# A two-pass form of 44 projection units, with the low half copied by ScalarE and added by VectorE

## The chip, the cores and the metric

The kernel runs on one core of a Trainium2 chip. The metric is the device time of one execution in microseconds (us); it was measured in 3 runs, and the median is 1423.44 us. One execution was also recorded by the hardware profiler. Times within the trace count from the start of its span.

## The reference, cut to what matters

A sequence of 256 tokens with 1024 channels goes through two layers of one kind of block and then through a block of another kind, the **third block**. All is float32. Its mixing stage begins like this (the splits are of one projection):

```python
h = rmsnorm(x, norm_mix)
proj = h @ w_in                      # 1024 -> all projections
(z, xbc, dt_raw, lru_y, lru_x, q, k, v, ret_g, gate_pre) = jnp.split(proj, offsets, axis=-1)
xbc = silu(causal_dwconv(xbc, conv_w, conv_b))          # four taps
xb  = causal_dwconv(lru_x, lru_conv_w, lru_conv_b)      # four taps
...                                  # gates r, i from xb; u; an associative scan gives hs
y_lru = hs * gelu(lru_y)
qh, kh = rotary(q), rotary(k)        # retention
y_ret = norm(retention(qh, kh, v)) * silu(ret_g)
```

The three branch outputs (state space, LRU, retention) are each multiplied by a branch matrix, gated, summed, projected and added to x, and a feed-forward with a three-tap convolution follows.

## The kernel before, in words

**Numbers in two halves.** Every matrix product is made of rounded operands: a value is split in a high half (rounded to the format of TensorE) and a low half (what is left), and a product is high x high + low x high + high x low. All weights come in *units* of 128 x 1024 values. There are 461 units, in a ring of four buffers: SyncE loads `raw`, ScalarE rounds it to `w_hi` (`high`, L502 to L512, 1024 columns in one instruction), GpSimd subtracts to get `w_lo` (`low`, L477 to L481, in two halves), TensorE uses both and signals `unit_done`. `high` for a unit waits until TensorE is done with the unit four places earlier; ScalarE issues it inside its own hand-written order, between its other work.

**A projection unit.** `linear_unit` (L1204) makes 128 output channels for 256 tokens: 8 blocks of 128 input channels, and for each three matmuls of 256 columns (`mm3`, L1191 to L1193), 24 in all, into a *slot*. The four slots are the first halves (256 columns) of PSUM banks 4 to 7, used in turn. Before it writes a slot, TensorE waits for `slot_free` or `act_free`, which the engine that read the slot last gives. The activations' halves lie side by side in the buffer `both`: per block 256 columns high, then 256 columns low. `up_unit` (L1217) is the same product in another form, used in the feed-forwards: 8 matmuls of 512 columns multiply `w_hi` with both halves at once, so that the low part arrives in the second half of the bank (`low_part`), and 8 of 256 columns add `w_lo` x high to the slot (L1223, L1225). There ScalarE copies the low part to SBUF (`copy_low`, L584) and VectorE adds it to the slot (`add_low`, L1863). A PSUM bank is 512 columns wide.

**The order of the third block's mixing stage.** Each engine runs a list written out by hand; nothing is planned by a program. TensorE's order is:

1. 8 units for `lru_x`, one for dt (a `linear_unit`), 12 for `xbc`. For each of the 20, ScalarE takes the slot (`take`, L890: first a `high`, then the wait for the unit), writes middle tap times slot plus bias to SBUF (`middle_tap`, L899) and VectorE adds the three shifted taps from the slot (`shifted_taps`, L2232, three dependent instructions), then frees the slot with a small memset (L2238). Beside this, VectorE subtracts to get low halves (`parts_low`, L2281) and works out a softplus in small steps (L2247 to L2276); ScalarE makes the high halves (L903) and the Silu of finished `xbc` channels (L928). After the ninth `xbc` unit TensorE makes a cumulative sum that waits for the softplus result (L1606), which ScalarE copies out two units later.
2. Four rounds: one unit of the LRU's gates in four parts of six matmuls, each part with its own slot (Tanh by ScalarE, L970), four transposes (L1631), and one query unit. VectorE copied the query slot to `qk` right after the unit (L2329). In the same round run, in this order: VectorE L2319, L2326; ScalarE `decays` (L957 Exp, L960 Tanh); VectorE L2331, L2334. The fourth part of a gate unit uses the slot of the query unit before it.
3. Four key units (copied by VectorE, L2338), with square roots on ScalarE (L995), VectorE's products (L2345) and eight scans (L2349) beside them.
4. 8 units for `lru_y`: Gelu by ScalarE (L1013), product by VectorE (L2358), high and low half of it (L903, L2281).
5. Gate and branch products, the value and state-space stage, 8 units for `z`.
6. 8 units for `ret_g` (`gate_high`, Silu by ScalarE, L1049), with small products of the retention between them; VectorE here scales eight tiles (L2455) and makes their low halves (L2460).
7. The remaining gate and branch products and the output projection, then the feed-forward.

Of the kernel before, what the change touches and what calls it, by code (L numbers as in the profile page):

```python
# [154 lines left out]
def program(nc, t, per_trip, found, blocks=3):  # L155
    with ExitStack() as ctx:
# [335 lines left out]
        def _(act):  # L492
# [402 lines left out]

            def middle_tap(dst, tap, bias):
                s = take()
                act.wait_ge(init, 1)
                act.activation(dst, slot(s), ACT.Identity, scale=tap, bias=bias)\  # L899
                    .then_inc(pre_ready, d.inc(pre_ready))  # L900
# [62 lines left out]
            for b in range(4):  # L963
# [10 lines left out]
                d.skip(unit_done)  # L974
                next_slot()
                decays(b)

# [6 lines left out]
            for q in range(4):  # L984
                high()
                d.skip(unit_done)
                next_slot()
                load_segments(q)
                if q == 0:
                    act.wait_ge(m2_ready, d.next(m2_ready, 4))  # L990
                if q < 2:
                    for k in (2 * q, 2 * q + 1):
                        if k >= 2:
                            act.wait_ge(root_out, d.next(root_out))
                        act.activation(bank(2 + k % 2), a2("r", 2 * k * T, 2 * T), ACT.Sqrt, scale=0.25)\  # L995
                            .then_inc(root_ready, d.inc(root_ready))
# [51 lines left out]
            def gate_high(c):  # L1048
                act.activation(a2("xdt", c * T, T), slot(take()), ACT.Silu).then_inc(act_free, d.inc(act_free))  # L1049
# [130 lines left out]
        def _(pe):  # L1180
# [36 lines left out]
            def up_unit():  # L1217
# [3 lines left out]
                pe.wait_ge(slot_free, d.next(slot_free))  # L1221
# [48 lines left out]
            def last_two(hi, lo, c, ready):  # L1270
# [10 lines left out]
                token_rows(other, hi, lo, c + 1, 1, True).then_inc(unit_done, d.inc(unit_done))  # L1281

# [297 lines left out]
            linear_unit(h_hi, h_lo, hlo_ready)  # L1580
            for _ in range(3):
                linear_unit(h_hi, h_lo)
# [12 lines left out]
            for _ in range(CH - RING + 1):  # L1595
                linear_unit(h_hi, h_lo)
            for c in range(SSD_T):
                linear_unit(h_hi, h_lo, free=None if c == 3 else slot_free)
# [15 lines left out]
            for b in range(4):  # L1614
# [18 lines left out]
                linear_unit(h_hi, h_lo, free=act_free)  # L1633
            linear_unit(h_hi, h_lo, free=act_free)
            linear_unit(h_hi, h_lo, free=act_free)
# [7 lines left out]
            linear_unit(h_hi, h_lo, free=act_free)  # L1643
            linear_unit(h_hi, h_lo)
# [28 lines left out]
            for c in range(CH):  # L1673
                linear_unit(h_hi, h_lo, free=slot_free if c < RING else act_free)
# [71 lines left out]
            for h in range(RET_H):  # L1746
                linear_unit(h_hi, h_lo, free=act_free)
# [8 lines left out]
                linear_unit(h_hi, h_lo, free=act_free)  # L1756
# [59 lines left out]
        def _(dve):  # L1816
# [408 lines left out]

            def shifted_taps(dst, s, name, c, per, taps, final):
# [59 lines left out]
            for c in range(CH):  # L2286
                s = take()
# [6 lines left out]
            for c in range(SSD_T):  # L2294
                s = take()
# [17 lines left out]
            for b in range(4):  # L2313
# [8 lines left out]
                for half in range(2):  # L2322
# [5 lines left out]
                s = take()  # L2328
                dve.tensor_copy(a2("qk", b * T, T), slot(s)).then_inc(slot_free, d.inc(slot_free))  # L2329
# [5 lines left out]
                    .then_inc(m2_ready, d.inc(m2_ready))  # L2335
            for q in range(4):
                s = take()
                dve.tensor_copy(a2("qk", (RING + q) * T, T), slot(s)).then_inc(slot_free, d.inc(slot_free))  # L2338
# [13 lines left out]
            for c in range(CH):  # L2352
                d.skip(unit_done)
                next_slot()
# [5 lines left out]
                if c:  # L2360
                    parts_low(0, c - 1, bank(3 - c % 2, 0, T))
            parts_low(0, CH - 1, bank(3, 0, T))
# [393 lines left out]
```

## Time and profile before

| what | value |
|---|---|
| median of 3 runs | 1423.44 us (1423.15 to 1423.67) |
| the profiled execution | 1422.63 us, of which the span is 1420.8 us |
| TensorE busy | 1407.9 us, 99% of the span |
| GpSimd busy | 1183.3 us, 83% |
| ScalarE busy | 867.9 us, 61% |
| VectorE busy | 711.0 us, 50% |
| DMA | 256 MB, 180 GB/s |
| third block's mixing stage | about 830 to 1200 us of the span |

The times are sums over the whole span. An average of this kind hides that an engine may be early in one stage and the last to finish in another, so it has to be read stage by stage. The granted clock of TensorE is given as a share of its full speed.

### The profile page before, as it was taken

The page shows a single profiled execution, that of the slowest core. Times are in us where ns is not written, and L with a number is a line of the kernel's source. Part 1 is how long each engine was busy: PE and PEld are TensorE (multiplying, and loading weights), DVE is VectorE, ACT ScalarE, POOL GpSimd, SP SyncE. Part 2 cuts the span into 40 slices and gives each one's busy share as a digit, 9 for nine tenths or more (in the row PEclk, how much of TensorE's full clock was granted, in tenths as well). Part 3 has the DMA queues.
Part 4 walks back from the last instruction along what each step waited for, and adds up shares of the span by engine and source line. Part 5 has one row for each costly group of instructions (what it writes and reads, how often), then busy time and mean ns, then how long its engine had stood idle before and what let it go on. Part 6 is the DMA issues. An engine that isn't in the chain of part 4 may idle for free.

```text
span 1420.8 us, 25105 instructions
## 1 busy us (share of the span) xinstructions
PE 1407.9 (99%) x7866; PEld 1208.7 (85%) x7866; DVE 711.0 (50%) x1594; ACT 867.9 (61%) x1463; POOL 1183.3 (83%) x926
## 2 busy tenths in 40 slices
PE   9999999999999999999999999999999999999998
PEld 8877778888888777788888899998899888888887
DVE  4654454645555734446555565660863612544444
ACT  6655656666675655657666676854444545755555
POOL 5977687999969777888999979899676898799995
PEclk9999999999999999999999999999999999999999
DMA  7765455666557755565666656566544466566663
GB/s 255 222 189 151 135 183 158 199 201 191 186 171 209 225 155 145 165 179 159 207 191 192 190 179 193 165 204 198 167 141 134 151 207 184 163 200 193 192 188 93
DMA packets 140064, 256.09 MB, mean 180 GB/s; under 512 B 8192, under 2 KB 98896, under 8 KB 139600
## 3 DMA queue, kind: packets, MB, share of 16 engines
q1 hardware_dynamic: 128224, 244.61, 56.1%
q10 hardware_dynamic: 11760, 10.41, 2.8%
q8 instruction: 50, 0.82, 0.2%
q14 instruction: 30, 0.25, 0.1%
HBM read 253.89 MB, written 1.10 MB: 179 GB/s over the span
## 4 chain that ended last, share of the span: by engine, by line
PE 96%; DVE 2%; ACT 1%; DMA 0%; issue 0%; SPq 0%; ACTq 0%
PE psum L1191 21%; PE psum L1192 20%; PE psum L1193 20%; PE psum L1223 17%; PE psum L1225 9%; DVE arena L2405 1%; PE psum L1310 1%; PE psum L1376 1%; PE psum L1329 1%; PE psum L1320 1%; PE psum L1298 1%; PE psum L1689 0%; PE psum L1377 0%; PE psum L1337 0%; DMA arena<-in_x 0%; PE psum L1439 0%
## 5 line engine op out<-in xcount | busy, mean ns | idle before, releaser
L480 POOL TENSOR_TENSOR w_lo<-raw,w_hi 128x512 fp32r<-128x512 f32 x461 | 603.8, 1310 | 221.2 <-ACT w_hi L512 217.8
L512 ACT ACTIVATE w_hi<-raw 128x1024 fp32r<-128x1024 f32 x461 | 486.8, 1058 | 298.6 <-PE psum L1193 189.4
L481 POOL TENSOR_TENSOR w_lo<-raw,w_hi 128x512 fp32r<-128x512 f32 x461 | 610.4, 1324 | 0.0
L1223 PE MATMUL psum<-both,w_hi 128*128 128x512 f32 x1040 | 259.1, 391 | 0.0
L1223 PEld LDWEIGHTS psum<-both,w_hi 128*128 128x128 f32 x1040 | 190.7, 188 | 36.6
L1191 PE MATMUL psum<-w_hi,both 128*128 128x512 f32 (+1 forms) x544 | 212.3, 390 | 0.0
L1193 PE MATMUL psum<-w_lo,both 128*128 128x512 f32 (+1 forms) x544 | 205.7, 378 | 0.0
L1192 PE MATMUL psum<-w_hi,both 128*128 128x512 f32 (+1 forms) x544 | 205.4, 378 | 0.0
L1225 PEld LDWEIGHTS psum<-both,w_lo 128*128 128x128 f32 x1040 | 141.9, 190 | 10.1
L1863 DVE TENSOR_TENSOR psum<-psum,arena 128x256 f32<-128x256 f32 x136 | 58.6, 432 | 174.1 <-ACT arena L584 174.1
L1225 PE MATMUL psum<-both,w_lo 128*128 128x256 f32 x1040 | 145.0, 282 | 0.0
L1191 PE MATMUL psum<-both,w_hi 128*128 128x256 f32 x488 | 141.5, 290 | 0.0
L1193 PE MATMUL psum<-both,w_hi 128*128 128x256 f32 x488 | 138.0, 283 | 0.0
L1192 PE MATMUL psum<-both,w_lo 128*128 128x256 f32 x488 | 138.0, 283 | 0.0
L1191 PEld LDWEIGHTS psum<-w_hi,both 128*128 128x128 f32 x544 | 102.3, 188 | 27.0 <-issue 9.6
L1193 PEld LDWEIGHTS psum<-w_lo,both 128*128 128x128 f32 x544 | 102.4, 188 | 20.0
L1192 PEld LDWEIGHTS psum<-w_hi,both 128*128 128x128 f32 x544 | 102.5, 189 | 17.4
L1191 PE MATMUL psum<-w_hi,f_hi 128*128 128x512 f32 x272 | 106.7, 392 | 0.0
L1192 PE MATMUL psum<-w_hi,f_lo 128*128 128x512 f32 x272 | 106.6, 392 | 0.0
L1193 PE MATMUL psum<-w_lo,f_hi 128*128 128x512 f32 x272 | 105.8, 389 | 0.0
L1191 PE MATMUL psum<-w_hi,y_hi 128*128 128x512 f32 x256 | 101.0, 394 | 0.0
L1193 PE MATMUL psum<-w_lo,y_hi 128*128 128x512 f32 x256 | 99.8, 390 | 0.0
(291 smaller groups left out, 2156.8 us busy)
## 6 DMA issues: line engine op xcount, KB each, us to landing
raw<-in_units SPq DMA_DIRECT2D x453, 512.0 KB, 3.6
arena<-gate_rows ACTq DMA_DIRECT2D x8, 512.0 KB, 7.6
raw<-in_units SPq DMA_DIRECT2D x8, 384.0 KB, 3.0
arena<-in_bias ACTq DMA_DIRECT2D x2, 1024.0 KB, 5.0
arena<-acs_rows ACTq DMA_DIRECT2D x16, 128.0 KB, 3.9
arena<-in_consts ACTq DMA_DIRECT2D x1, 1296.0 KB, 6.0
raw<-in_units SPq DMA_DIRECT2D x8, 128.0 KB, 3.0
out<-arena SPq DMA_DIRECT2D x4, 256.0 KB, 2.7
```

What stands on the lines that cost most here:

```text
L480: pool.tensor_tensor(w_lo[s][:, 0:D // 2], raw[s][:, 0:D // 2], w_hi[s][:, 0:D // 2].bitcast(F32), ALU.subtract)
L481: pool.tensor_tensor(w_lo[s][:, D // 2:D], raw[s][:, D // 2:D], w_hi[s][:, D // 2:D].bitcast(F32), ALU.subtract)\
L512: act.activation(w_hi[s][:, :], raw[s][:, :], ACT.Copy).then_inc(hi_ready, d.inc(hi_ready))
L1191: pe.matmul(out, hi, r_hi, start=start, stop=False, **kw)
L1192: pe.matmul(out, lo, r_hi, start=False, stop=False, **kw)
L1193: return pe.matmul(out, hi, r_lo, start=False, stop=stop, **kw)
L1223: pe.matmul(bank(4 + k), blocks_of(w_hi[s], c), both[:, 2 * c * T:2 * (c + 1) * T], start=(c == 0), stop=False, skip_group_check=True)
L1225: last = pe.matmul(slot(k), blocks_of(w_lo[s], c), chunk(h_hi, c), start=False, stop=(c == CH - 1), skip_group_check=True)
L1298: last = pe.matmul(turned_chunk(c, half * P, P), tok(x, half, c * P, P), rows[:, half * P:(half + 1) * P], start=True, stop=True)
L1310: last = pe.matmul(bank(h, r * T, T), arena[lo:hi, at:at + P], arena[lo:hi, ak:ak + T], start=True, stop=True)
L1320: last = pe.transpose(bank(2, kc * T + r * P, P), sc[:, r * T + kc * P:r * T + (kc + 1) * P], ident)
L1863: dve.tensor_tensor(slot(k), slot(k), low_part(k)[1], ALU.add).then_inc(vec, d.inc(vec))
```

## The change

The units of steps 1 (without dt), 2, 3, 4 and 6 take the form of `up_unit`: 8 + 12 + 4 + 4 + 8 + 8 = 44. The dt unit, the `z` units, the gate and branch products stay. `up_unit` gets a parameter for the signal it waits for. The very first unit is written out with a wait before each block (`first_unit`).

What reads the slots changes with it. `take_sum` on ScalarE is `take`, then a copy of the low part to `pre` (SBUF), then a wait for VectorE's sum; `take_sum` on VectorE waits for that copy and adds it to the slot. It is used for the convolution units, the Gelu units and the Silu units; the operation on the slot follows the sum. For queries and keys ScalarE copies the slot (the high part) to `qk` (`query_part`) and VectorE adds the low part straight from PSUM (`query_sum`). In step 2 the query copy stands behind `decays`, and VectorE's addition at the end of its round instead of in its middle. In step 4 `parts_low` moves from behind the product to before it, one unit later.

```diff
+            def take_sum():            # ScalarE
+                s = take()
+                act.activation(chunk(pre, s), low_part(s)[0], ACT.Copy).then_inc(low_out, d.inc(low_out))
+                act.wait_ge(sum_ready, d.next(sum_ready))
+                return s
+            def query_part(c):
+                act.wait_ge(unit_done, d.next(unit_done))
+                act.activation(a2("qk", c * T, T), slot(next_slot()), ACT.Copy).then_inc(low_out, d.inc(low_out))
             def middle_tap(dst, tap, bias):
-                s = take()
+                s = take_sum()
...
-                d.skip(unit_done)
-                next_slot()
                 decays(b)
+                query_part(b)
...
                 high()
-                d.skip(unit_done)
-                next_slot()
+                query_part(RING + q)
                 load_segments(q)
...
-                    act.activation(a2("merged", c * T, T), slot(take()), ACT.Gelu_apprx_tanh).then_inc(act_free, d.inc(act_free))
+                    act.activation(a2("merged", c * T, T), slot(take_sum()), ACT.Gelu_apprx_tanh).then_inc(act_free, d.inc(act_free))
...
-                act.activation(a2("xdt", c * T, T), slot(take()), ACT.Silu).then_inc(act_free, d.inc(act_free))
+                act.activation(a2("xdt", c * T, T), slot(take_sum()), ACT.Silu).then_inc(act_free, d.inc(act_free))
...
+            def first_unit():          # TensorE
+                s = unit()
+                k = next_slot()
+                pe.wait_ge(slot_free, d.next(slot_free))
+                for c in range(CH):
+                    pe.wait_ge(hlo_ready, d.next(hlo_ready))
+                    pe.matmul(bank(4 + k), blocks_of(w_hi[s], c), both[:, 2 * c * T:2 * (c + 1) * T], start=(c == 0), stop=False, skip_group_check=True)
+                    last = pe.matmul(slot(k), blocks_of(w_lo[s], c), chunk(h_hi, c), start=False, stop=(c == CH - 1), skip_group_check=True)
+                last.then_inc(unit_done, d.inc(unit_done))
...
-                linear_unit(h_hi, h_lo, free=None if c == 3 else slot_free)
+                up_unit(free=None if c == 3 else slot_free)
...
-                linear_unit(h_hi, h_lo, free=act_free)
+                up_unit(free=act_free)
...
+            def take_sum():            # VectorE
+                s = take()
+                dve.wait_ge(low_out, d.next(low_out))
+                dve.tensor_tensor(slot(s), slot(s), chunk(pre, s), ALU.add).then_inc(sum_ready, d.inc(sum_ready))
+                return s
+            def query_sum(c):
+                s = take()
+                dve.wait_ge(low_out, d.next(low_out))
+                dve.tensor_tensor(a2("qk", c * T, T), a2("qk", c * T, T), low_part(s)[0], ALU.add).then_inc(slot_free, d.inc(slot_free))
...
-                s = take()
+                s = take_sum()
                 shifted_taps(a2("xbc", c * T, T), s, "ssd_conv", c, 5, 4, conv_done)
...
-                s = take()
-                dve.tensor_copy(a2("qk", b * T, T), slot(s)).then_inc(slot_free, d.inc(slot_free))
                 dve.wait_ge(a_ready, d.next(a_ready))
...
                     .then_inc(m2_ready, d.inc(m2_ready))
+                query_sum(b)
             for q in range(4):
-                s = take()
-                dve.tensor_copy(a2("qk", (RING + q) * T, T), slot(s)).then_inc(slot_free, d.inc(slot_free))
+                query_sum(RING + q)
...
             for c in range(CH):
-                d.skip(unit_done)
-                next_slot()
+                take_sum()
+                if c >= 2:
+                    parts_low(0, c - 2, bank(2 + c % 2, 0, T))
                 dve.wait_ge(act_free, d.next(act_free))
...
                 for _ in range(2):
-                    d.skip(unit_done)
-                    next_slot()
+                    take_sum()
                 dve.wait_ge(act_free, d.next(act_free, 2))
```

## Rows read from the trace of the kernel before

**Rows 1.** The page, part 4: the chain that ended last, by engine.
```profile
PE 96%; DVE 2%; ACT 1%; DMA 0%; issue 0%; SPq 0%; ACTq 0%
```
**Rows 2.** Windows: stretch, its length, busy time of PE, PEld, DVE, ACT, POOL; clock.
```profile
833.00:893.00 60.00, 60.00 (x496) 59.10 (x495) 36.09 (x100) 40.06 (x65) 55.60 (x44) 1.00 0.63 201
```
**Rows 3.** Waits of VectorE, 833 to 960: total us, times, longest.
```profile
DVE arena L2232 <- ACT arena L899: 23.3, 18, 4.9
```
**Rows 4.** Timeline of ScalarE, second convolution group: start, duration, line, operation.
```profile
868.07 1.28 ACT L928 ACT_TABLE_LOAD   x1
...
876.13 0.57 ACT L899 ACTIVATE arena<-psum,prm 128x256 f32<-128x256 f32 x1 [1.06 <-PE psum L1193]
...
876.90 1.05 ACT L512 ACTIVATE w_hi<-raw 128x1024 fp32r<-128x1024 f32 x1
879.01 0.57 ACT L899 ACTIVATE arena<-psum,prm 128x256 f32<-128x256 f32 x1 [1.06 <-PE psum L1193]
...
885.70 0.57 ACT L899 ACTIVATE arena<-psum,prm 128x256 f32<-128x256 f32 x1 [2.00 <-PE psum L1193]
```
**Rows 5.** Timeline of TensorE: the cumulative sum; two units of the feed-forward.
```profile
881.78 0.61 PE L1606 MATMUL psum<-arena 128*16 128x256 f32 x2
...
1264.66 1.98 PE L1223 MATMUL psum<-both,w_hi 128*128 128x512 f32 x8
...
1270.22 0.40 PE L1191 MATMUL psum<-w_hi,f_hi 128*128 128x512 f32 x1
```
**Rows 6.** Groups of instructions, whole span, then 833 to 893: busy us, mean ns.
```profile
L1863 DVE TENSOR_TENSOR psum<-psum,arena 128x256 f32<-128x256 f32 x136 | 58.6, 432 | 174.1 <-ACT arena L584 174.1
L584 ACT ACTIVATE arena<-psum 128x256 f32<-128x256 f32 x136 | 49.4, 367 | 3.7 <-PE psum L1225 3.7
...
L2268 DVE SCALAR_TENSOR_TENSOR rows<-rows,psum 128x40 f32<-128x40 f32 x7 | 1.4, 195 | 0.2
```
**Rows 7.** Timeline of VectorE: three taps, a low half, the longest softplus step.
```profile
844.70 1.52 DVE L2232 SCALAR_TENSOR_TENSOR arena<-psum,prm,arena 128x255 f32<-128x255 f32 x3 [1.36 <-ACT arena L899]
846.15 0.99 DVE L2281 TENSOR_TENSOR y_lo<-arena,y_hi 128x512 fp32r<-128x512 f32 x1
...
878.25 0.82 DVE L2272 SCALAR_TENSOR_TENSOR psum<-rows,rstd 128x40 f32<-128x40 f32 x1
```
**Rows 8.** Timeline of GpSimd: first half of the weights rounded at 876.90.
```profile
878.96 1.30 POOL L480 TENSOR_TENSOR w_lo<-raw,w_hi 128x512 fp32r<-128x512 f32 x1
```
**Rows 9.** Timelines of TensorE, ScalarE and VectorE, one gate round (907 to 915).
```profile
907.16 0.60 PE L1631 MATMUL psum<-common,arena 128*128 128x128 f32 x4
...
913.36 0.60 PE L1631 MATMUL psum<-common,arena 128*128 128x128 f32 x4
...
908.11 0.82 ACT L970 ACTIVATE arena<-psum,prm 128x256 f32<-128x256 f32 x2
...
910.47 1.10 ACT L957 ACTIVATE arena<-arena,small 128x256 f32<-128x256 f32 x2 [0.58 <-DVE arena L2319]
...
908.96 1.47 DVE L2319 SCALAR_TENSOR_TENSOR arena<-arena 128x512 f32<-128x512 f32 x1 [0.84 <-ACT arena L970]
...
911.60 1.81 DVE L2331 TENSOR_TENSOR psum<-arena 128x512 f32<-128x512 f32 x1 [0.17 <-ACT arena L957]
913.44 0.69 DVE L2334 SCALAR_TENSOR_TENSOR arena<-psum,arena 128x512 f32<-128x512 f32 x1
```
**Rows 10.** Timelines of ScalarE, VectorE and GpSimd at the first LRU gate units.
```profile
932.57 0.38 ACT L1013 ACTIVATE arena<-psum 128x256 f32<-128x256 f32 x1 [0.46 <-PE psum L1193]
932.86 1.05 ACT L512 ACTIVATE w_hi<-raw 128x1024 fp32r<-128x1024 f32 x1
...
933.54 2.33 DVE L2349 TENSOR_TENSOR_SCAN arena<-arena 128x256 f32<-128x256 f32 x2
...
936.93 1.47 POOL L480 TENSOR_TENSOR w_lo<-raw,w_hi 128x512 fp32r<-128x512 f32 x1
```
**Rows 11.** Timeline of VectorE, retention gates: the last low halves of the long run.
```profile
1079.61 1.29 DVE L2460 TENSOR_TENSOR y_lo<-arena,y_hi 128x512 fp32r<-128x512 f32 x2
```

More of the change, by code:

```diff
@@ L1215, in linear_unit, with up_unit @@
                 last.then_inc(unit_done, d.inc(unit_done))
-            def up_unit():
+            def up_unit(free=slot_free):
                 s = unit()
                 k = next_slot()
-                pe.wait_ge(slot_free, d.next(slot_free))
+                if free is not None:
+                    pe.wait_ge(free, d.next(free))
                 for c in range(CH):
@@ L1579, in _ @@
             turn_norm()
-            linear_unit(h_hi, h_lo, hlo_ready)
+            first_unit()
             for _ in range(3):
-                linear_unit(h_hi, h_lo)
+                up_unit()
             def linear_units(n, src_hi=h_hi, src_lo=h_lo):
@@ L1593, in turn_rows @@
                 last.then_inc(turn_ready, d.inc(turn_ready))
-            for _ in range(CH - RING + 1):
-                linear_unit(h_hi, h_lo)
+            for _ in range(CH - RING):
+                up_unit()
+            linear_unit(h_hi, h_lo)
             for c in range(SSD_T):
-                linear_unit(h_hi, h_lo, free=None if c == 3 else slot_free)
+                up_unit(free=None if c == 3 else slot_free)
                 if c == 0:
@@ L1632, in _ @@
                 last.then_inc(xt_ready, d.inc(xt_ready))
-                linear_unit(h_hi, h_lo, free=act_free)
-            linear_unit(h_hi, h_lo, free=act_free)
-            linear_unit(h_hi, h_lo, free=act_free)
+                up_unit(free=act_free)
+            up_unit(free=act_free)
+            up_unit(free=act_free)
             pe.wait_ge(silu_ready, d.next(silu_ready, SSD_T - CH))
@@ L1642, in _ @@
                 last.then_inc(cb_ready, d.inc(cb_ready))
-            linear_unit(h_hi, h_lo, free=act_free)
-            linear_unit(h_hi, h_lo)
+            up_unit(free=act_free)
+            up_unit()
             def column_part(hi, lo, part, pair):
@@ L1673, in _ @@
             for c in range(CH):
-                linear_unit(h_hi, h_lo, free=slot_free if c < RING else act_free)
+                up_unit(free=slot_free if c < RING else act_free)
             gate_columns(act_free)
@@ L1746, in _ @@
             for h in range(RET_H):
-                linear_unit(h_hi, h_lo, free=act_free)
+                up_unit(free=act_free)
                 if h == 0:
@@ L1755, in _ @@
                     last.then_inc(sbc_ready, d.inc(sbc_ready))
-                linear_unit(h_hi, h_lo, free=act_free)
+                up_unit(free=act_free)
                 if h >= 2:
@@ L2294, in _ @@
             for c in range(SSD_T):
-                s = take()
+                s = take_sum()
                 shifted_taps(a2("xbc", c * T, T), s, "ssd_conv", c, 5, 4, conv_done)
@@ L2359, in _ @@
                     .then_inc(prod_ready, d.inc(prod_ready))
-                if c:
-                    parts_low(0, c - 1, bank(3 - c % 2, 0, T))
-            parts_low(0, CH - 1, bank(3, 0, T))
+            for m in (CH - 2, CH - 1):
+                parts_low(0, m, bank(2 + m % 2, 0, T))
             def free_gates():
```

1 line of the change is left out of this document (removed).

## The prediction

> **What bounds the kernel now.** I read the page first: of the chain that ended last 96% is TensorE [rows 1]. So a microsecond taken out of TensorE's work is a microsecond of time, as long as nothing else becomes late; a wait put into TensorE's stream costs its full length, since no later slack takes it back. Next the stage that the change touches. In the 60 us of the two convolution groups TensorE is busy throughout, VectorE for 36 and ScalarE for 40 [rows 2]. That looks like room. But the waits of VectorE say what its idle time is: it waits 18 times for ScalarE's middle tap, 23.3 us in all over the stage [rows 3]. It is idle because it is early; the question is whether it stays early.
>
> **What is gained.** A unit in the old form takes TensorE 2.88 us: two middle taps, each released by its unit, start at 876.13 and 879.01 [rows 4]. The new form is already in the feed-forward stage: two such units take 5.56 us from 1264.66 to 1270.22 [rows 5], so 2.78 each. The columns are the same (24 x 256 against 8 x 512 + 8 x 256); eight issues per unit fall away. 0.10 x 44 = **4.4 us gained**. The granted clock is 1.00 in the stage [rows 2], the 2.4 GHz level, and nothing here lowers it for long. The Trainium skill ("TensorE: Matmul & The Clock Gate", Back-to-back issue gap) gives a gap of N/2.4 + 2.5 ns for one warm matmul; an estimate by that page makes the gain 0.02 us per unit and 0.9 us in all. The rows have loads of weights between the matmuls and decide; the page's figure is a rival below.
>
> **What is added.** Per summed unit a ScalarE copy of 0.37 us and a VectorE addition of 0.43 us, both with rows of the same kind and shape [rows 6]. For the eight query and key units VectorE's copy becomes an addition of about the same length, and ScalarE gets one copy of 0.37 more. The busy time fits. What doesn't fit so easily is the order, since both engines work through theirs strictly in turn.
>
> **Convolution units (20).** Now the tap on ScalarE starts as the unit ends, and VectorE's three taps follow. In the new order: copy 0.36, hop, addition 0.43, hop, middle tap 0.57 [rows 4], hop, three taps of 1.45 in all, from 844.70 to 846.15 [rows 7]. Hops are 0.05 to 0.09 (a middle tap at 876.13 to 876.70, VectorE's taps 0.1 later; I take 0.05 towards ScalarE and 0.1 back). The result is 0.84 later. Worse, VectorE adds unit c+1 only after the taps of c, and then waits for ScalarE's tap: its turn is 0.43 + 0.05 + 0.57 + 0.1 + 1.45 + 0.05 = 2.65 us against TensorE's 2.78. The spare 0.13 is all that is left for the rest of VectorE's work, which lay in the 23.3 us: four subtractions of about 1.0 (one stands in [rows 7]), and the softplus steps, 4.4 us busy and 4.7 with their gaps (seven of 0.195 [rows 6], one of 0.82 [rows 7], ten others of 0.15 to 0.41).
> - First group, 8 units: VectorE needs 8 x 2.65 + 3 x 1.0 = 24.2, TensorE 22.2: 2.0 late. The dt unit gives VectorE a pause, but ScalarE must first wait for the last taps, then load a table; it goes into the second group 2.7 late.
> - Second group to the end of the softplus (7 units): VectorE 18.6 + 1.0 + 4.7 = 24.3, and 0.4 for ScalarE's table load of 1.28 and its Silus, which now stand behind a late tap [rows 4]; TensorE 19.8. That makes 2.7 + 4.9 = 7.6 late.
> - How much is free? ScalarE is blocked on the sum, and behind it stands the rounding of the next weights, then GpSimd's subtraction. The rounding at 876.90 [rows 4] was taken up by GpSimd at 878.96, and its two halves of 1.3 were done at 881.5 [rows 8]; TensorE began that unit at 885.5, just before the tap at 885.70. With 1.05 + 2.56 for the two steps it could have started 4.9 later; 0.75 of this is a small product that stands there alone, 0.3 goes with the faster units, 0.84 with the longer path. 3.0 is left. So TensorE waits 7.6 - 3.0 = 4.6, rounded up to 5.1 for the cumulative sum, which waits for the softplus result (written by 879.4, two short steps after the 0.82 of [rows 7]; used at 881.8 [rows 5]) and was only 2.4 us behind it; part of the wait is late weights, part this.
> - The cumulative sum is copied by ScalarE two units before it is turned, behind a late tap as well: 0.9.
> Sum 6.0. Bounds: 2 (hops of nothing and subtractions of 0.8) to 9 (hops of 0.1 both ways).
>
> **Gate units (4).** The fourth part of each takes the slot of a query unit. VectorE freed it by a copy right after the unit; now ScalarE copies behind the decays, and VectorE adds at the end of its round. Read it in one round [rows 9]: the gate unit is done at 907.16; the last step before the new addition ends at 913.44 + 0.69 = 914.13, so the slot is free at 914.6. The next gate unit was done at 913.36, its fourth part (six matmuls, 0.72) began at 912.64. The first such wait is 2.0. Then TensorE's stall pulls its own chain along: from the start R of a fourth part, the last Tanh is done at R + 1.4, the scaling (1.47) at 2.9, the exponentials (1.10) at 4.05, the square (1.81) at 5.9, the next step (0.69) at 6.6, the addition at 7.05 [rows 9]; TensorE is back at R + 0.72 + 0.44 + 2.78 + 2.16 = 6.1. So 0.9 for each of the other two. The very first gate unit needs the slot of the last convolution unit, and that comes out of VectorE 0.84 and some 1.1 late, before 0: 2.0. Sum 2.0 + 2.0 + 0.9 + 0.9 = 5.8; bounds 3.5 (steady waits gone) to 8 (every wait as long as the first).
>
> **Queries, keys and the scans.** The additions are where the copies were. ScalarE's segment loads (eight transfers on its queue) and its square roots now come behind the query copy, 0.4 later; the loads are needed only in the value stage, two stages on, which hides them, and they would cost that 0.4 if needed at once. Then come eight LRU gate units, whose sums stand behind VectorE's scans. There a rounding starts at 932.86, 0.3 after the Gelu of a finished unit at 932.57; TensorE wants those weights three units of 2.88 after that unit's end, at 941.0, and with 1.05 and GpSimd's two halves of 1.47 [rows 10] the rounding could slip by 4.0. In the new order it stands behind the last scans, which end at 933.54 + 2.33 = 935.9 [rows 10], behind the addition and the Gelu: it moves to 936.7, by 3.8. VectorE is besides 2.1 later against TensorE than now: 0.8 for copy and addition ahead of the roots, 0.7 where ScalarE's third query copy stands behind a root and a rounding, 0.1 for longer additions, 0.5 for five faster units. 5.9 - 4.0 = **1.9 us**, bounds 0 (only the 3.8 counts) and 4. The subtraction of the high part (0.43), moved ahead of the product, falls into VectorE's pause for the Gelu.
>
> **Gates of the retention (8 units).** One VectorE run of subtractions ends at 1080.9 [rows 11]; the additions of the next units stand behind it, and the rounding behind them on ScalarE slips by some 1.5 (this row and the hops), of the 3.0 that are free. Cost 0, and 1.5 if that slack were gone. The first unit with its waits per chunk: 0.
>
> **Sum.** 6.0 + 5.8 + 1.9 = 13.7 of waits, less 4.4: **+9.3**. On the profiled execution: 1420.8 + 9.3 = 1430.1 of span, and 1.8 around it: 1431.9. That execution (1422.63) lies 0.8 under the median, so the forecast is **1432.7**.
>
> **The rivals.**
> - *Faster: VectorE keeps up.* If all lateness stays below the 3.0 and the slots are not missed, only 4.4 comes out: 1419.0. For it: VectorE is busy for 60% of the stage [rows 2], and ScalarE's copy with VectorE's addition is hidden in the feed-forward. Against: there VectorE doesn't do three taps and a softplus in each unit, and in the gate stage the addition's place is simply later than the slot's need. 7%.
> - *Only the gate slots count.* The convolution lag stays under 3.0 (turn of 2.5 in place of 2.65), the gates cost 5.8 or somewhat less, the scans 0 to 1: 1423.44 + 5.8 + 0.5 - 4.4 = 1425.3 (1423 to 1428). 15%.
> - *Worse: contention.* The subtractions out of SBUF stretch GpSimd's and their own time (the square took 1.81 in the round shown), and a later schedule lays them over each other; with hops of 0.1 on both ways too: 3 to 5 more, 1437. The Trainium skill ("SBUF — State Buffer", SBUF: two separate sides) says that a VectorE operation with two SBUF inputs locks out GpSimd's. The added additions have one input in PSUM, so by that page they add none. 12%.
> - *The new form gives nothing here* (it runs at the pace of the old one, or the skill's gap holds): waits as above, gain 0 to 0.9, 1436 to 1437. The row of the feed-forward speaks against it. 3%.
> My forecast has the remaining 63%, with 1428 to 1437 as its own range.
>
> **How the numbers follow.** The kernel's runs agree so well that over 0.2%, 2.8 us, can be told from none. Slower by more (over 1426.3): forecast, contention, no gain, and a part of the gate-slot case, 0.84. Within: the greater part of that case, 0.09. Faster: 0.07. The range leaves out the faster case and the far end of contention: 1424.5 to 1438.5.
>
> **What would show it.** Right: TensorE units of 2.78 us; TensorE idle before weights in the second convolution group (about 3 us), at the product for the cumulative sum (2 to 3), at each fourth gate part (2, 2, 1, 1), and once in the LRU gate units; VectorE's wait for the middle tap some 0.7 in each unit instead of 1.3; ScalarE waiting for VectorE's sums. Wrong: fewer than 5 us of TensorE idle in the stage (then the turn of VectorE is shorter than summed here), or waits in the retention gates, which I cost at nothing.

## The result and the profile after

The changed kernel takes 1433.1 us (median of 4 runs, 1431.16 to 1433.71), the kernel before on the same chip 1423.3 us (4 runs, 1422.97 to 1423.67). The ratio is 1.0067, with an interval of 1.0055 to 1.0079: slower by 9.8 us by the medians. The forecast was 1432.7. The profiled execution took 1433.55 us, with a span of 1431.8, 11.0 more than before. Of these 1.1 lie ahead of the stage (the norm's sum begins at 826.15 in place of 825.06); that is no sign of the change, since over the traces of all runs this start lies anywhere from 824.5 to 826.2, in the changed kernel's second trace (experiment 8) at 825.5. From the norm's sum to the end of the stage it is 294.7 us in place of 284.8: the stage itself grew by 9.9.

The page of the changed kernel: busy time (part 1) and the chain that ended last (part 4).
```profile
PE 1407.9 (98%) x7514; PEld 1191.4 (83%) x7514; DVE 723.1 (51%) x1630; ACT 881.1 (62%) x1507; POOL 1181.0 (82%) x926
...
PE 87%; DVE 4%; ACT 4%; issue 3%; POOL 2%; DMA 1%; PEld 0%; ACTq 0%; POOLq 0%; DVEq 0%; PEldq 0%; SPq 0%
```
TensorE is busy for as long as before, over a longer span. VectorE and ScalarE gained 12 to 13 us of work each, which is little against their idle time, and GpSimd none (1183.3 before); yet the chain, 96% TensorE before [rows 1], now leaves it for VectorE and ScalarE. That is the mark of waits in TensorE's stream, and the view of its waits names them (826 to 1125; total us, times, longest):
```profile
PE psum L1201 <- DVE arena L2261: 2.5, 2, 1.9
PE psum L1630 <- DVE small L2313: 2.4, 1, 2.4
PE psum L1201 <- DVE small L2275: 1.9, 1, 1.9
PE psum L1234 <- POOL w_lo L481: 1.6, 1, 1.6
PE psum L1713 <- DVE arena L2445: 1.3, 4, 0.8
PE psum L1321 <- ACT rows L530: 0.7, 1, 0.7
PE psum L1766 <- ACT arena L1055: 0.7, 1, 0.7
PE psum L1201 <- POOL w_lo L481: 0.6, 1, 0.6
```
In the order of this list: slots of gate units that the query sum (L2261) frees late; the cumulative sum, late for the last softplus step (L2313); a gate unit on the slot of the last convolution unit (memset L2275); late weights; L1713, which the kernel before had as well, at 1.2 us; the norm ahead of the stage, which the form alone has too (before, it falls just outside this window); a product of the retention; and late weights at the first gate product behind the Gelu units. Where they fall, in the timeline of TensorE:
```profile
877.91 2.11 PE L1234 MATMUL psum<-both,w_hi 128*128 128x512 f32 x8 [1.63 <-POOL w_lo L481]
...
886.13 0.59 PE L1630 MATMUL psum<-arena 128*16 128x256 f32 x2 [2.36 <-DVE small L2313]
...
889.78 2.00 PE L1234 MATMUL psum<-both,w_hi 128*128 128x512 f32 x8
...
892.57 2.00 PE L1234 MATMUL psum<-both,w_hi 128*128 128x512 f32 x8
...
900.12 0.39 PE L1201 MATMUL psum<-y_hi,w_hi 128*128 128x256 f32 x1 [1.87 <-DVE small L2275]
...
908.42 0.39 PE L1201 MATMUL psum<-y_hi,w_hi 128*128 128x256 f32 x1 [1.92 <-DVE arena L2261]
...
923.10 0.39 PE L1201 MATMUL psum<-y_hi,w_hi 128*128 128x256 f32 x1 [0.62 <-DVE arena L2261]
...
970.96 0.50 PE L1201 MATMUL psum<-w_hi,both 128*128 128x512 f32 x1 [0.57 <-POOL w_lo L481]
...
1092.55 1.05 PE L1766 MATMUL psum<-arena 128*128 128x1 f32 x8 [0.68 <-ACT arena L1055]
```
Two units follow each other in 892.57 - 889.78 = 2.79 us. The waits that are new add up to 1.6 + 2.4 + 1.9 + 1.9 + 0.6 + 0.6 + 0.7 = 9.7 us. Why they are there is seen on VectorE, right behind the cumulative sum (timeline):
```profile
888.42 0.06 DVE L2275 MEMSET small<- 128x1 f32 x1
888.55 0.43 DVE L2254 TENSOR_TENSOR psum<-psum,pre 128x256 f32<-128x256 f32 x1
889.62 1.51 DVE L2269 SCALAR_TENSOR_TENSOR arena<-psum,prm,arena 128x255 f32<-128x255 f32 x3 [0.63 <-ACT arena L911]
891.08 0.06 DVE L2275 MEMSET small<- 128x1 f32 x1
891.21 0.43 DVE L2254 TENSOR_TENSOR psum<-psum,pre 128x256 f32<-128x256 f32 x1
```
The addition starts as the memset ends, so VectorE is behind and not waiting for work. Still it idles for 0.63 us, because the tap on ScalarE needs its sum and its own taps need that tap. The turn is 891.21 - 888.55 = 2.66 us, against TensorE's 2.79. The windows (columns as in [rows 2]) show no engine full:
```profile
833.00:893.00 60.00, 55.95 (x324) 48.59 (x323) 40.61 (x110) 42.43 (x77) 51.96 (x40) 1.00 0.55 181
...
904.00:908.00 4.00, 2.50 (x21) 2.30 (x20) 2.20 (x6) 3.99 (x8) 4.00 (x3) 1.00 0.30 105
908.00:912.00 4.00, 3.58 (x16) 3.10 (x17) 2.17 (x5) 3.74 (x7) 2.94 (x3) 0.69 0.47 157
912.00:916.00 4.00, 4.00 (x29) 3.76 (x28) 2.88 (x3) 2.36 (x6) 3.17 (x3) 0.88 0.34 131
```
VectorE is busy for 41 of 60 us while TensorE waits for it. The last rows show something for which the prediction's sum had no term ("nothing here lowers it for long"): a granted clock of 0.69 after two waits of 1.9 us. TensorE ran there for a while at 1.2 GHz, and the unit from 909.66 to 914.05 took 4.4 us, where the one of the round before, from 901.30 to 904.18, took 2.9.

### The profile page after: what moved, and what is told of

The parts are those of the page before. It is cut to its first block, busy times and chain, and to the rows that moved or that the text cites. A ratio compares the mean times of both kernels' runs of the same rounds, so it can differ in the third digit from the quotient of the medians.

```text
span 1431.8 us, 24524 instructions
## 1 busy us (share of the span) xinstructions
PE 1407.9 (98%) x7514; PEld 1191.4 (83%) x7514; DVE 723.1 (51%) x1630; ACT 881.1 (62%) x1507; POOL 1181.0 (82%) x926
## 4 chain that ended last, share of the span: by engine, by line
PE 87%; DVE 4%; ACT 4%; issue 3%; POOL 2%; DMA 1%; PEld 0%; ACTq 0%; POOLq 0%; DVEq 0%; PEldq 0%; SPq 0%
PE psum L1234 19%; PE psum L1201 17%; PE psum L1203 17%; PE psum L1202 17%; PE psum L1236 10%; DVE arena L2269 1%; DVE arena L2440 1%; PE psum L1333 1%; PE psum L1399 1%; POOL w_lo L481 1%; PE psum L1352 1%; PE psum L1343 1%; POOL w_lo L480 1%; ACT w_hi L512 1%; ACT arena L911 1%
## 5 line engine op out<-in xcount | busy, mean ns | idle before, releaser
L512 ACT ACTIVATE w_hi<-raw 128x1024 fp32r<-128x1024 f32 x461 | 486.7, 1058 | 297.8 <-PE psum L1203 190.5
L1234 PE MATMUL psum<-both,w_hi 128*128 128x512 f32 x1384 | 348.3, 394 | 1.7 <-POOL w_lo L481 1.6
L1234 PEld LDWEIGHTS psum<-both,w_hi 128*128 128x128 f32 x1384 | 253.6, 189 | 50.5 <-POOL w_lo L481 2.3
L1236 PEld LDWEIGHTS psum<-both,w_lo 128*128 128x128 f32 x1384 | 188.9, 190 | 13.7
L1236 PE MATMUL psum<-both,w_lo 128*128 128x256 f32 x1384 | 192.9, 282 | 0.0
L1202 PE MATMUL psum<-w_hi,y_lo 128*128 128x512 f32 x256 | 99.6, 389 | 0.0
L826 ACT ACTIVATE pre<-psum,prm 128x256 f32<-128x256 f32 x88 | 49.3, 563 | 25.6 <-DVE psum L1891 25.5
L1891 DVE TENSOR_TENSOR psum<-psum,rstd 128x256 f32<-128x256 f32 x136 | 58.5, 432 | 4.8
```

The costliest lines, as they stand in the source:

```text
L512: act.activation(w_hi[s][:, :], raw[s][:, :], ACT.Copy).then_inc(hi_ready, d.inc(hi_ready))
L826: act.activation(pre[:, (2 * b + k) * T:(2 * b + k + 1) * T], slot(2 * b + k), ACT.Identity, scale=at(1), bias=at(3)).then_inc(pre_ready, ...
L1202: pe.matmul(out, lo, r_hi, start=False, stop=False, **kw)
L1234: pe.matmul(bank(4 + k), blocks_of(w_hi[s], c), both[:, 2 * c * T:2 * (c + 1) * T], start=(c == 0), stop=False, skip_group_check=True)
L1236: last = pe.matmul(slot(k), blocks_of(w_lo[s], c), chunk(h_hi, c), start=False, stop=(c == CH - 1), skip_group_check=True)
L1891: dve.tensor_tensor(slot(k), slot(k), rstd[:, :], ALU.mult).then_inc(sum_ready, d.inc(sum_ready))
```

## The experiments

The first theory was that of the prediction: the copy and the addition shift or block the order of ScalarE and VectorE, and each late signal costs TensorE its length. The rivals were contention (the load of the extra operations, whatever their order) and a form that gains nothing. The ratios are against the kernel before as it was measured beside each group of runs: 1422.88 us for experiments 1 to 4, 1423.02 for 5 to 8, 1422.90 for 9 to 11.

**1. The form alone.** The units keep the two passes, but nothing copies or adds the low half. The change of `take_sum` on ScalarE, with VectorE's and the queries in the same manner:
```diff
             def take_sum():
                 s = take()
-                act.activation(chunk(pre, s), low_part(s)[0], ACT.Copy).then_inc(low_out, d.inc(low_out))
-                act.wait_ge(sum_ready, d.next(sum_ready))
                 return s
```


> All 44 units keep the two-pass form on TensorE, but the low half is neither copied nor added, and queries are copied by VectorE at their old place; the part high weights x low activations is left out of the result. My theory (the form gains 0.10 us per unit, everything lost is waits): 1418.9 us, 4.4 under the kernel before, within 1418.4 to 1419.8. Rival, the form itself gains nothing because it runs at the pace of the old one: 1423.3. Rival by the Trainium skill's gap of N/2.4 + 2.5 ns: 1422.4.

Measured 1419.98 us (1418.93 to 1421.19), ratio 0.9978 [0.9968, 0.9988]. Of the waits of TensorE in the stage these are left, both without a share in the change (L1711 is the L1713 of above):
```profile
PE psum L1711 <- DVE arena L2439: 1.4, 5, 0.7
PE psum L1319 <- ACT rows L530: 0.7, 1, 0.7
```
So the form gives 2.9 us by the medians, a little less than the range expected, and by the trace the stage shrinks from 284.8 to 281.3 us: 3.5 / 44 = 0.08 per unit in place of 0.10 (the later expectations reckon with 0.077). The rest is what copying and adding cost: 1433.1 - 1420.0 = 13.1 us by the medians (12.7 if each is taken against the kernel before of its own group), 13.3 by the two traces. Summed were 13.7.

**2. The four queries of the rounds in the old form.**
```diff
+                d.skip(unit_done)
+                next_slot()
                 decays(b)
-                query_part(b)
...
-                up_unit(free=act_free)
+                linear_unit(h_hi, h_lo, free=act_free)
...
+                s = take()
+                dve.tensor_copy(a2("qk", b * T, T), slot(s)).then_inc(slot_free, d.inc(slot_free))
...
-                query_sum(b)
```


> The changed kernel with only the four query units of the gate rounds back in the old form (copied by VectorE in the middle of its round). My theory, the place of the addition makes the fourth gate part wait: the waits of 1.9, 0.1 and 0.6 us and the stretch at half clock that follows the first (1.6 us) go, 0.4 of gain goes with them: 1433.1 - 3.8 = 1429.3, within 1428.5 to 1430.8. Rival, added load as such (four copies and additions of 88): 1432.5 to 1433.1.

Measured 1429.73 us (1429.21 to 1430.35), 1.0049 [1.0032, 1.0065]. Only L2261's waits are gone from the list of TensorE, the others are as long as before. The windows:
```profile
904.00:908.00 4.00, 3.99 (x34) 3.78 (x33) 1.83 (x4) 3.99 (x8) 3.48 (x3) 1.00 0.41 131
908.00:912.00 4.00, 4.00 (x35) 4.00 (x35) 2.90 (x5) 3.71 (x8) 3.75 (x3) 1.00 0.47 131
```
The wait is gone and so is the stretch at the lower clock. The slots are a cause of their own.

**3. The 20 convolution units in the old form.**
```diff
             def middle_tap(dst, tap, bias):
-                s = take_sum()
+                s = take()
...
-            first_unit()
+            linear_unit(h_hi, h_lo, hlo_ready)
             for _ in range(3):
-                up_unit()
+                linear_unit(h_hi, h_lo)
...
```


> The changed kernel with only the 20 convolution units back in the old form, without copy and addition. My theory: the waits for weights (1.6), for the softplus result (2.4), at the turn of the sums (0.3) and for the slot of the last convolution unit (1.9) go, 2.0 of gain goes with them: 1433.1 - 4.2 = 1428.9, within 1427.9 to 1430.2. A load theory (20 of 44 parts of 14.2 us lost, less 2.0) gives 1428.6, so this run alone does not tell them apart; the trace does, by whether VectorE is early again.

Measured 1427.37 us (1426.12 to 1428.72), 1.0032 [1.0019, 1.0044], 0.5 below the range expected and 5.7 below the changed kernel. In the profiled execution, one of the two fastest, the stage is 6.8 us shorter than in the changed kernel. The gates' own wait stands in TensorE's timeline as long as ever, and the clock around it is 1.00:
```profile
902.37 0.39 PE L1201 MATMUL psum<-y_hi,w_hi 128*128 128x256 f32 x1 [1.94 <-DVE arena L2261]
```
So the two groups of waits are nearly independent. What comes back beyond them is the stretch at the lower clock, which is gone here too: the last 1.6 of the 6.8 us come in the third and fourth round. There, at full clock, the fourth parts of the gate units wait for 0.36 us and not at all.

**4. The same load, without the tap's wait for it.** VectorE adds after the tap, into a buffer that nothing reads (the low part of these 20 units is left out of the result).
```diff
             def middle_tap(dst, tap, bias):
-                s = take_sum()
+                s = take()
+                act.activation(chunk(pre, s), low_part(s)[0], ACT.Copy).then_inc(low_out, d.inc(low_out))
...
+            def take_beside():         # VectorE, in place of take_sum for the 20
+                s = take()
+                dve.wait_ge(low_out, d.next(low_out))
+                dve.wait_ge(pre_ready, d.value(pre_ready, "wait", -1))
+                dve.tensor_tensor(chunk(pre, s), slot(s), chunk(pre, s), ALU.add).then_inc(vec, d.inc(vec))
+                return s
```


> The changed kernel with the same copies and additions for the 20 convolution units, but ScalarE's middle tap no longer waits for the sum: VectorE adds after the tap, into another buffer, so the low part is left out of the result of these units. The load is the same, only the wait between the two engines is gone. My theory (VectorE's turn falls from 2.65 to about 2.0 us, so it stays early): the waits of 6.2 us go, at most 0.5 of them stays: 1426.9 to 1427.6. Rival, the load of the additions and copies or their contention with GpSimd is what costs: unchanged, 1432.5 to 1433.5.

Measured 1424.91 us (1424.2 to 1426.88), 1.0017 [1.0008, 1.0027]. As many copies and additions run as in the changed kernel, and yet the waits for weights at L1234 and for the softplus are gone, and of the 1.9 for the last convolution slot 0.5 is left:
```profile
PE psum L1202 <- DVE arena L2269: 2.3, 2, 1.9
...
PE psum L1202 <- POOL w_lo L481: 0.6, 1, 0.6
PE psum L1202 <- DVE small L2283: 0.5, 1, 0.5
```
TensorE reaches the cumulative sum 55.35 us after the norm's sum, as in the form alone (55.32), against 59.98 in the changed kernel. This run decides between order and load in the convolution units: what costs there is that VectorE's taps stand behind ScalarE's tap, which stands behind VectorE's sum. The time itself was missed, by 2.0 below the range expected: that range left the stretch at the lower clock in, and here the clock stayed at 1.00, which is worth 1.5 us in the third and fourth round.

**5 to 7. The sum one unit earlier.** If the turn is the trouble, VectorE could add unit c+1 before the taps of c; ScalarE's tap would then find its sum ready.
```diff
+            ahead = take_sum()
             for c in range(SSD_T):
-                s = take_sum()
+                s = ahead
+                if c < SSD_T - 1:
+                    ahead = take_sum()
                 shifted_taps(a2("xbc", c * T, T), s, "ssd_conv", c, 5, 4, conv_done)
                 release()
```
The first run has this in both groups, the second has it with the rounds' queries in the old form as in experiment 2:

> The changed kernel, but in the 20 convolution units VectorE adds the low half of unit c+1 before it makes the taps of unit c. Copies, additions and waits are all there, only the order on VectorE differs. My theory (VectorE's turn of 2.65 us falls to about 2.05, since it no longer stands idle for ScalarE's middle tap): the waits for weights and for the softplus result go, about 0.9 us stays at the slot of the last convolution unit (its taps end 0.84 later), the waits of the gate rounds stay: as in the run without the wait, a little more, 1425.3, within 1424.3 to 1427. Rival, the load or contention of the additions: 1432 to 1433.5.

> As before it (the low half of unit c+1 added ahead of the taps of unit c), and the four query units of the gate rounds in the old form. My theory by the parts measured so far: 40 units x 0.077 = 3.1 us gained; left are 0.9 at the last convolution slot, 0.9 behind the scans, 1.3 among the retention gates: 1422.9 - 3.1 + 3.1 = 1422.9, within 1421.9 to 1423.9, no different from the kernel before. Rival, that some of the loss belongs to the load of 80 copies and additions: 1425 or more.

The third keeps the new form only where it seemed free: 19 convolution units and the four keys.

> The two-pass form only where the earlier runs found cover: 8 + 11 convolution units with the addition ahead of the taps of the unit before, and the four key units. The last convolution unit, the query units of the rounds, the Gelu and the Silu units have the old form. My theory: 23 x 0.077 = 1.8 us gained and no wait: 1421.1, within 1420.4 to 1422.0. Rival, waits move to a place not seen so far: 1422.5 to 1424.

Measured 1441.39 (1440.67 to 1443.71), 1440.15 (1439.65 to 1441.41) and 1437.97 us (1436.46 to 1438.73), ratios 1.0127 [1.011, 1.0144], 1.0121 [1.0104, 1.0138] and 1.0106 [1.009, 1.0123]. All three lie 14 us or more above the theory's range, and far above the rivals too (that of the second run had named only "1425 or more"). The timeline of ScalarE in the first of them:
```profile
880.28 0.56 ACT L911 ACTIVATE arena<-psum,prm 128x256 f32<-128x256 f32 x1 [0.57 <-DVE psum L2254]
881.69 0.42 ACT L940 ACTIVATE arena<-arena 128x256 f32<-128x256 f32 x1 [0.85 <-DVE arena L2269]
...
882.97 0.36 ACT L899 ACTIVATE pre<-psum 128x256 f32<-128x256 f32 x1
883.89 0.56 ACT L911 ACTIVATE arena<-psum,prm 128x256 f32<-128x256 f32 x1 [0.57 <-DVE psum L2254]
```
and of VectorE beside it:
```profile
879.81 0.43 DVE L2254 TENSOR_TENSOR psum<-psum,pre 128x256 f32<-128x256 f32 x1 [2.84 <-ACT pre L899]
880.15 1.50 DVE L2269 SCALAR_TENSOR_TENSOR arena<-psum,prm,arena 128x255 f32<-128x255 f32 x3
```
ScalarE's list was left as it was. Behind the tap of unit c it holds the Silu of the channel before (L940), which needs that channel's last taps on VectorE, and these now stand behind the addition of unit c. Until then ScalarE can't copy the next low half, for which VectorE waits 2.84 us. The cycle didn't go away, it moved, and it got longer: 883.89 - 880.28 = 3.61 us on ScalarE. TensorE's waits show the price (the two longest groups, same columns as above):
```profile
PE psum L1630 <- DVE small L2313: 4.6, 1, 4.6
PE psum L1234 <- POOL w_lo L481: 3.2, 3, 1.8
```

**8. The changed kernel again**, unedited, to see whether the lower clock is a matter of chance.

> The changed kernel once more, for the stretch at a lower granted clock after the two waits of 1.9 us at the gate rounds. My theory, it belongs to the waits that lie close together there and not to chance: the trace has it again at the same place, 1.0 to 1.6 us long in cost, and the time is 1433.1 within 1431.5 to 1434. Rival, a chance of one execution: no such stretch and 1431.5 or less in most runs.

Measured 1432.55 us (1431.11 to 1432.97), 1.0063 [1.0046, 1.008]. The new waits have the same lengths, and the windows have the stretch at the same place:
```profile
908.00:912.00 4.00, 4.00 (x16) 3.48 (x16) 2.03 (x4) 3.85 (x8) 3.39 (x3) 0.57 0.49 131
```

**9 to 11. Both lists reordered.** The sum one unit early, as in 5, and on ScalarE the work that needs finished taps moved one unit later, between the copy of the low half and the wait for the sum; the softplus steps one unit earlier.
```diff
-            def take_sum():
+            def take_sum(between=lambda: None):
                 s = take()
                 act.activation(chunk(pre, s), low_part(s)[0], ACT.Copy).then_inc(low_out, d.inc(low_out))
+                between()
                 act.wait_ge(sum_ready, d.next(sum_ready))
...
-                middle_tap(a2("xbc", c * T, T), p2("ssd_conv", c * 5 + 3), p2("ssd_conv", c * 5 + 4))
+                def silus():
+                    if c == 4:
+                        xbc_silu(0)
+                        xbc_silu(1)
+                    if c >= 4:
+                        xbc_silu(c - 2)
+                middle_tap(a2("xbc", c * T, T), p2("ssd_conv", c * 5 + 3), p2("ssd_conv", c * 5 + 4), silus)
...
-                if c == 3:
-                    xbc_silu(0)
-                    xbc_silu(1)
-                if c >= 3:
-                    xbc_silu(c - 1)
...
```


> What the run with the early addition missed is mended: on ScalarE the Silu and the rounding of finished convolution channels come one unit later and stand between the low copy and the wait for the sum, so that ScalarE no longer waits for taps that VectorE now makes later; the softplus steps come one unit earlier. VectorE adds unit c+1 before the taps of c. The rest is the changed kernel. My theory (nobody's turn is over 2.78 us: VectorE 2.05 and its small steps, ScalarE 2.3): waits for weights and for the softplus result go, 0.9 stays at the last convolution slot, the gate rounds stay: 1425.4, within 1424.4 to 1427. Rival, the additional hops through two engines cost in any order: 1430 or more.

Measured 1427.05 us (1426.47 to 1429.46), 1.003 [1.002, 1.004]: 6.0 less than the changed kernel. ScalarE's timeline now:
```profile
876.95 0.37 ACT L899 ACTIVATE pre<-psum 128x256 f32<-128x256 f32 x1
877.21 0.41 ACT L942 ACTIVATE arena<-arena 128x256 f32<-128x256 f32 x1
878.10 0.56 ACT L912 ACTIVATE arena<-psum,prm 128x256 f32<-128x256 f32 x1 [0.47 <-DVE psum L2258]
...
879.51 0.37 ACT L899 ACTIVATE pre<-psum 128x256 f32<-128x256 f32 x1
```
The Silu fills the time in which the sum is made, and a turn is 879.51 - 876.95 = 2.56 us. TensorE reaches the cumulative sum 55.3 us after the norm's sum, against 60.0 in the changed kernel and 56.7 in the one before. Of the waits for weights and for the softplus none is left (as the softplus steps moved too, this run doesn't tell their share); the slots are (TensorE's timeline, then the window behind the second row):
```profile
892.83 0.39 PE L1205 MATMUL psum<-y_hi,w_hi 128*128 128x256 f32 x1 [1.10 <-DVE small L2279]
...
902.56 0.39 PE L1205 MATMUL psum<-y_hi,w_hi 128*128 128x256 f32 x1 [1.92 <-DVE arena L2265]
...
904.00:908.00 4.00, 4.00 (x15) 3.27 (x15) 3.41 (x4) 3.08 (x6) 4.00 (x4) 0.57 0.41 131
```
The lower clock is back too, in its place. Together with 1.6 us at the last convolution slot (1.1 and 0.5) in place of the 0.9 reckoned, it accounts for the 1.6 above what had been expected. Next, this order with the rounds' queries in the old form as in experiment 2, and last the new form in 19 convolution units and the keys alone (rest old):

> As before it, with the four query units of the rounds in the old form. My theory: 40 units x 0.077 = 3.1 gained, 3.1 of waits left (0.9 last convolution slot, 0.9 behind the scans, 1.3 in the retention gates): 1422.9, within 1421.9 to 1423.9. Rival: 1426 or more, if waits move on.

> As before it, and the last convolution unit, the Gelu and the Silu units in the old form as well: the two-pass form in 19 convolution and 4 key units, with the reordered engines. My theory: 23 x 0.077 = 1.8 us gained and no wait left: 1421.2, within 1420.4 to 1422.0, faster than both kernels. Rival, a wait not foreseen eats it: 1422.5 to 1424.

Measured 1424.49 (1423.51 to 1425.9), 1.0011 [1.0002, 1.0021], and 1422.03 us (1421.06 to 1424.74, 11 runs), 0.9995 [0.9986, 1.0004]. Both miss: the first lies 0.6 above its range, and the second at the very edge of its own, not faster than both kernels as expected. In the first one the wait at the last convolution slot is 1.6 in place of 0.9, and behind it stands a lower clock:
```profile
896.00:900.00 4.00, 4.00 (x26) 4.00 (x25) 1.81 (x3) 3.97 (x6) 3.13 (x3) 0.69 0.15 60
```
Its executions spread over more than the length of that stretch: four with a mean granted clock of 1.000 took 1423.5 to 1424.6 us, four of the other six, at 0.998 or 0.999, 1425.6 to 1425.9. In the second one a single wait with a part in the change is left:
```profile
PE psum L1208 <- DVE small L2285: 0.4, 1, 0.4
```
Its stage is 283.7 us long, 1.1 shorter than before (in an execution of 1421.17 us, 0.9 below the median), and by its time it can't be told from the kernel before. It is 11 us faster than the changed kernel. A better place for the query's addition, right after the unit on VectorE, wasn't tried.

## Why the prediction was right

It forecast +9.3 us and +9.8 came. The stretches of the stage hold the steps against the measurement. The cost is the changed kernel less the form alone, from the starts of TensorE's operations in the two traces; between the norm's sum and the cumulative sum, for instance, 60.0 less 55.3.

| stretch | predicted | measured | TensorE waits in it |
|---|---|---|---|
| to the cumulative sum | 5.1 | 4.7 | 1.6, 2.4 |
| to its turn | 0.9 | 0.2 | under 0.3 |
| to the first gate unit's transposes | 2.0 | 2.1 | 1.9 |
| second round | 2.0 | 2.2 | 1.9 |
| third round | 0.9 | 1.2 | none over 0.3; lower clock |
| fourth round | 0.9 | 0.9 | 0.6 |
| queries' end to the state-space stage | 1.9 | 0.9 | 0.6 |
| state space | 0 | 0.2 | none |
| gates of the retention | 0 | 1.0 | 0.7 |
| sum (before rounding) | 13.7 | 13.3 | 9.7 |

- *The gain* was mis-sized: 3.5 instead of 4.4. The row of two units in the feed-forward [rows 5] read 2.78; here they come at 2.79, and where another product stands ahead, eight matmuls take 2.09 to 2.11 instead of 2.00. Between the form alone and the kernel before, the 17 units up to the cumulative sum gained 0.08 each, the three between the transposes of the rounds 0.05 each. The rival of no gain falls. The gap formula of the Trainium skill ("TensorE: Matmul & The Clock Gate", Back-to-back issue gap) would have made the gain 0.9 in all, an estimate by that page, which gives the formula for a single isolated matmul; the traces of this stream don't agree with it.
- *VectorE's turn* was right to a hundredth: 2.65 summed, 2.66 read, with a wait for the tap of 0.63 (said: 0.7). The convolution units cost 4.9 for 6.0. The split was as forecast: part late weights (1.6), part the softplus result (2.4). The 5.1 to the cumulative sum held 0.5 that no step of the sum gave (4.6, "rounded up"); 4.7 came. Too high was the guess for the cumulative sum's turn, 0.9 for 0.2. Experiment 4 shows the mechanism itself.
- *The gate slots:* 6.4 for 5.8, in the order 1.9, 1.9, almost none, 0.6 where 2, 2, 1, 1 was said. The first two terms hold within 0.2. The two steady waits of 0.9 were mis-sized, and luck hid it: where the clock stayed at 1.00 (experiments 3 and 4) the third and fourth round wait 0.36 and nothing, and cost 0.5 to 0.6 over the form alone, not 1.8. In the changed kernel they cost 2.1, because a unit at half clock, which the prediction didn't have, brought 1.5 more. By experiments 2 and 3 the terms of the slots and of the convolution units add up: each can be taken away alone.
- *The Gelu units* cost less and later than said: the wait isn't in them, but comes as 0.57 for weights at the first gate product. GpSimd got the rounded weights late there (1.74 us of waiting for L512 at 968.37), which fits the slipped rounding that was named as the cause. The wait is gone in the form alone and in experiment 11, where these units are old.
- *The retention gates* were a miss, 0 predicted and 1.0 measured; the prediction had itself named waits there as a sign of being wrong. The argument looked only at the slack of the weights. Behind the sum stands another signal on ScalarE as well (timeline of ScalarE, changed kernel):
```profile
1089.97 0.36 ACT L899 ACTIVATE pre<-psum 128x256 f32<-128x256 f32 x1
1091.60 0.38 ACT L1059 ACTIVATE arena<-psum 128x256 f32<-128x256 f32 x1 [1.26 <-DVE psum L2254]
1091.88 0.62 ACT L1055 ACTIVATE arena<-arena 128x512 f32<-128x512 f32 x1
```
ScalarE waits 1.26 us for a sum, the square (L1055) comes after it, and TensorE's small product at 1092.55 needs that square. In experiment 11, with these units old, this wait is gone.
- *Contention* as a rival: no cost of it was seen. An addition takes 0.43 as before, GpSimd's busy time didn't rise, and experiment 4, with the full load, has no wait in the convolution units. The longest softplus step did take 1.18 in place of 0.82, but 1.09 in the form alone too, without any addition.

By the traces the stage grew by 9.86 us, 0.56 more than the sum: the gain was 0.92 too high, the costs 0.36 too high. Inside the costs the terms miss by up to 1.0 in both directions and cancel, and 1.5 us of them come from a lower clock that stood in no term. So the hit to half a microsecond owes much to luck; its sign and rough size don't.

## What to carry to other kernels

Where two engines work strictly in turn and hand each other something in each unit, sum the whole round trip, with the hops, and set it against the unit's period: here 2.66 us of round trip in a period of 2.79 left nothing, though both engines were busy for less than three quarters of the time. A change of order on one engine alone moved this cycle to the other; both lists changed together opened it, with work of the other kind between the handing over and the wait. And before an operation is added behind a signal, list everything that stands behind it on its engine: slots, roundings, and the small squares that some product wants.

## What the runs showed of the hardware

Waits of less than 2 us were followed by a lower TensorE clock. In the changed kernel two waits of 1.9 us, with 6.4 us between them, are followed by a granted clock of 0.69 and 0.57 in the windows of its two traces; in experiment 9 waits of 1.1, 0.5 and 1.9 are, by 0.57. After a single wait of 1.9 (experiments 2 and 3) it stayed at 1.00. In experiment 5 it fell behind a wait of 1.8 in late weights: eight matmuls of 512 columns that take 2.00 otherwise took 3.67:
```profile
868.23 3.67 PE L1234 MATMUL psum<-both,w_hi 128*128 128x512 f32 x8 [1.77 <-POOL w_lo L481]
```
The length of the waits alone doesn't decide it. In experiment 6 the same wait for weights, of 1.75, left the clock at 1.00, and the eight matmuls behind it took 2.14; in experiment 10 the waits of 1.1 and 0.5 at the last convolution slot are followed by 0.69, in experiment 9 the same two at the same place by 1.00. What sets it off stays open. Its price was 1.5 to 1.6 us each time in the gate rounds, on top of the waits: from the start of the fourth part to the end of the unit behind it TensorE took 914.05 - 908.42 = 5.63 us, and a round earlier 904.18 - 900.12 = 4.06. And a unit's gain from merged passes was smaller than two units of another stage had said: 0.08 us on average, not 0.10.
